# An odd layer's latent projections as three products of fp32r parts in place of float32 products

## The reference

```python
c_q, c_kv, k_r = jnp.split(t @ w_in, (MLA_Q_LORA, MLA_Q_LORA + MLA_KV_LORA), axis=-1)
...
return jnp.split(_heads(c_q @ w_uq, MLA_HEADS, MLA_NOPE_DIM + MLA_ROPE_DIM), (MLA_NOPE_DIM,), axis=-1)
...
k_nope, v = jnp.split(_heads(c_kv @ w_ukv, MLA_HEADS, MLA_NOPE_DIM + MLA_V_DIM), (MLA_NOPE_DIM,), axis=-1)
k_shared = jnp.broadcast_to(k_r[:, None], k_nope.shape[:-1] + (MLA_ROPE_DIM,))
...
y = _merge_heads(_dense_attention(q[:, :, None], k, v, kc, vc, MLA_SCALE)[:, :, 0]) @ w_out
```

## Time and profile before

| | us |
|---|---|
| median of 3 runs (2413.46 to 2417.34) | 2415.53 |
| the profiled execution, its own time | 2413.82 |
| its span | 2412.4 |
| PE busy (matmul) | 2257.8 |
| DVE busy | 1271.6 |
| ACT busy | 1074.9 |
| mean granted clock of TensorE, share of full speed | 0.973 |

### The profile page before, as it was taken

The page is one execution under the profiler, slowest core; times in us unless marked ns, Lnnn a source line. Parts: engine busy times, 40 slices in busy tenths (PEclk is TensorE's granted clock), DMA queues, the critical chain, the costliest instruction groups (busy, mean ns, idle before and its releaser), DMA issues.

```text
span 2412.4 us, 39225 instructions
## 1 busy us (share of the span) xinstructions
PE 2257.8 (94%) x17014; PEld 2017.2 (84%) x17014; DVE 1271.6 (53%) x1928; ACT 1074.9 (45%) x1691; POOL 54.2 (2%) x100
## 2 busy tenths in 40 slices
PE   6999979998999999989996989999999999998997
PEld 5998869997999799879995766888888886477997
DVE  3555566556555666365555326763444653446665
ACT  3444455445444554354435526552333451345553
POOL 0000100000000000000000000000000000000000
PEclk9999989999999999989998999999999999999998
DMA  7454625545554544245444121022223433204451
GB/s 313 175 192 184 228 107 206 195 170 197 185 200 166 205 188 166 108 183 189 183 158 193 70 74 49 1 105 87 88 101 126 158 123 136 74 18 156 165 200 39
DMA packets 51627, 353.58 MB, mean 147 GB/s; under 512 B 8064, under 2 KB 8448, under 8 KB 8832
## 3 DMA queue, kind: packets, MB, share of 16 engines
q1 hardware_dynamic: 47520, 346.05, 38.4%
q10 hardware_dynamic: 864, 4.63, 0.5%
q0 software_dynamic: 3072, 0.40, 0.1%
HBM read 349.61 MB, written 1.05 MB: 145 GB/s over the span
## 4 chain that ended last, share of the span: by engine, by line
PE 85%; DVE 8%; ACT 4%; DMA 1%; issue 1%; SPq 0%; POOL 0%; DVEq 0%; ACTq 0%
PE ps L683 13%; PE ps L685 13%; PE ps L684 13%; PE ps L818 5%; PE ps L2381 5%; PE ps L2383 5%; PE ps L2382 4%; PE ps L383 3%; PE ps L384 2%; PE ps L385 2%; PE ps L2111 2%; PE ps L2112 2%; PE ps L2113 2%; PE ps L1347 1%; PE ps L884 1%; PE ps L871 1%
## 5 line engine op out<-in xcount | busy, mean ns | idle before, releaser
L358 DVE TENSOR_TENSOR wl<-ring,wh 128x1024 fp32r<-128x1024 f32 x406 | 477.5, 1221 | 276.0 <-ACT wh L353 275.4
L683 PE MATMUL ps<-xs,wh 128*128 128x256 f32 x1760 | 504.5, 287 | 24.8 <-DVE wl L358 13.9
L684 PE MATMUL ps<-xs,wl 128*128 128x256 f32 x1760 | 503.2, 286 | 0.0
L685 PE MATMUL ps<-xs,wh 128*128 128x256 f32 x1760 | 503.1, 286 | 0.0
L353 ACT ACTIVATE wh<-ring 128x1024 fp32r<-128x1024 f32 x406 | 405.1, 1050 | 177.8 <-PE ps L685 128.0
L683 PEld LDWEIGHTS ps<-xs,wh 128*128 128x128 f32 x1760 | 343.6, 195 | 28.3 <-issue 18.9
L684 PEld LDWEIGHTS ps<-xs,wl 128*128 128x128 f32 x1760 | 343.4, 195 | 0.0
L685 PEld LDWEIGHTS ps<-xs,wh 128*128 128x128 f32 x1760 | 343.2, 195 | 0.0
L683 PE MATMUL ps<-hh,wh 128*128 128x256 f32 x880 | 249.1, 283 | 0.7 <-DVE hl L784 0.7
L684 PE MATMUL ps<-hh,wl 128*128 128x256 f32 x880 | 249.0, 283 | 0.0
L685 PE MATMUL ps<-hl,wh 128*128 128x256 f32 x880 | 249.0, 283 | 0.0
(11 more groups left out here) (426 smaller groups left out, 4004.5 us busy)
## 6 DMA issues: line engine op xcount, KB each, us to landing
ring<-wstream SPq DMA_DIRECT2D x329, 1024.0 KB, 4.9
ada_rows<-ada_stage POOLq DMA_DIRECT2D x96, 4.0 KB, 4.3
CN<-consts ACTq DMA_DIRECT2D x1, 1136.0 KB, 15.7
X<-xin ACTq DMA_DIRECT2D x1, 1024.0 KB, 10.7
X<-cin ACTq DMA_DIRECT2D x1, 1024.0 KB, 9.2
out<-X SPq DMA_DIRECT2D x1, 1024.0 KB, 3.9
PT__65<-pin ACTq DMA_DIRECT2D x1, 512.0 KB, 18.9
ab_w<-wab ACTq DMA_DIRECT2D x1, 512.0 KB, 3.7
```

The lines of the kernel that those rows point to most:

```text
L358: dve.tensor_tensor(lo, tile_of(i), hi.bitcast(F32), ALU.subtract).then_inc(low_part, 1)
L683: pe.matmul(out, wh[:, w, c, :], x_hi, start=start, stop=False, skip_group_check=True)
L684: pe.matmul(out, wl[:, w, c, :], x_hi, start=False, stop=False, skip_group_check=True)
L685: return pe.matmul(out, wh[:, w, c, :], x_lo, start=False, stop=True, skip_group_check=True)
```

## The change

- The x half's norm no longer writes `H` but parts: `act_x_high` makes the high part of a tile and a new `act_whole` the whole value, both on ACT, two instructions a tile where one stood; DVE subtracts (`dve_modulated_low`, L579 of the old file). The context half's norm is split in the same way, with the whole value on DVE.
- The 13 weight slots of `l1_in`, `l1_uq` and `l1_ukv` are split slot by slot: `act_m_high(s)` on ACT, `dve_m_low(s)` on DVE, the latter into the ring slot. Slots 0 to 3, 11 and 12 have 2048 columns, slot 4 has 256, slots 5 to 10 have 1536. From slot 6 on, and for slots 2 to 4, the high part waits for the products of an earlier slot. Slots 0 and 1 are split among the last feed-forward pieces, slots 2 to 6 among the `l1_in` tiles, 7 to 12 among the `l1_uq` tiles and the rotary chain.
- The scaled latents are split too: three ACT copies and one DVE subtraction for `c_q`, two copies and one subtraction for `c_kv`. ACT comes to the two copies behind the second query tile, and DVE waits for them before it turns and spreads `k_r`.
- PE forms three fp32r products where it formed one in float32, over the same chunks and tiles; the sums of squares, the rotations, the attention and `l1_out` stay in float32.

The diff, cut to its core:

```diff
-           "l0_1x": "l0_x", "l0_1c": "l0_c", "l1_1": "l1"}
+           "l0_1x": "l0_x", "l0_1c": "l0_c", "l0_2x": "l1_x", "l0_2c": "l1_c", "l1_1": "l1"}
...
-            if name in ("l0_1x", "l0_1c"):
+            if name[0:2] == "l0":
...
-            for c in (2 * q, 2 * q + 1):
+            for c in (2 * q, 2 * q + 1) if name != "l0_2x" else ():
...
+        M_SLOTS = ([("l1_in", j, 2 * KC * P) for j in range(4)] + [("l1_in", 4, KC * ROPE)]
+                   + [("l1_uq", j, 12 * P) for j in range(6)] + [("l1_ukv", j, 2 * KC * P) for j in range(2)])
+        m_wh = [put("m_wh", [2, SLOT], F32R, ("big", 16384)), put("m_wh1", [1, SLOT], F32R, ("Z", 8192)),
+                put("m_wh2", [2, SLOT], F32R, ("XH", 0))]
+        m_w_high, m_w_low = sem("m_w_high"), sem("m_w_low")
+
+        def m_load(s):
+            return FIRST[M_SLOTS[s][0]] + M_SLOTS[s][1]
+
+        def m_high(s):
+            k, j = (0, s % 2) if s < 5 else (1, 0) if s == 5 else (2, s % 2)
+            return m_wh[k][:, j, 0:M_SLOTS[s][2]]
+
+        def m_low(s):
+            return ring_low[:, m_load(s) % RING, 0:M_SLOTS[s][2]]
+
+        def m_parts(s, kc, width):
+            return (w[:, 0:kc * width].rearrange("p (c m) -> p c m", c=kc) for w in (m_high(s), m_low(s)))
+
+        def act_m_high(s):
+            act.wait_ge(*loaded(m_load(s)))
+            if s < 2:
+                act.wait_ge(f_low, NPAIR + 7)
+            elif s == 5:
+                act.wait_ge(*x_split("l1_c"))
+                act.wait_ge(x_high, x_parts("l1_c") + 4)
+            else:
+                act.wait_ge(raw_done, FREED[m_load(4 if s == 6 else s - 2)][1])
+            act.activation(m_high(s), slot(m_load(s))[:, 0:M_SLOTS[s][2]], ACT.Copy).then_inc(m_w_high, 1)
+
+        def dve_m_low(s):
+            dve.wait_ge(m_w_high, s + 1)
+            dve.tensor_tensor(m_low(s), slot(m_load(s))[:, 0:M_SLOTS[s][2]], m_high(s).bitcast(F32), ALU.subtract
+                              ).then_inc(m_w_low, 1)
...
-                    act_modulated("l0_2x", 2 * (k - 6))
-                    act_modulated("l0_2x", 2 * (k - 6) + 1)
+                    for c in (2 * (k - 6), 2 * (k - 6) + 1):
+                        act_x_high("l0_2x", c)
+                        act_whole("l0_2x", c)
+                if k in (7, 9):
+                    act_m_high(k // 8)
...
+            act.activation(x_whole(name, c), Z[:, ln_half(name), c, :], ACT.Identity, scale=g, bias=b).then_inc(low_whole, 1)
...
+                if k >= 7:
+                    dve_modulated_low("l0_2x", k - 7)
+                if k == 9:
+                    dve_m_low(0)
...
             dve_pair("l0_2c", 3, z + 16)
+            dve_m_low(1)
...
+            def tile(s, at, M, b, kc, hi, lo, N, width):
+
+                w_hi, w_lo = m_parts(s, kc, width)
+                pe.wait_ge(m_w_low, s + 1)
+                for c in range(kc):
+                    pe.matmul(ps[0:M, b, 0:N], w_hi[:, c, at:at + M], hi(c), start=(c == 0), stop=False)
+                    pe.matmul(ps[0:M, b, 0:N], w_lo[:, c, at:at + M], hi(c), start=False, stop=False)
+                    mm = pe.matmul(ps[0:M, b, 0:N], w_hi[:, c, at:at + M], lo(c), start=False, stop=(c == kc - 1))
+                mm.then_inc(raw_done, 1)
...
+            pe.wait_ge(*x_split("l1_x"))
+            for t in range(6):
+                tile(t // 2, (t % 2) * P, P, bank_cq(t), KC, half(0), half(1), T, 2 * P)
             pe.wait_ge(*m_a.at("cq5"))
-            total(m_cq_sq, 6, T, 4, "sum0")
-            pe.wait_ge(h_made, 2 * KC)
-            pe_raw_tiles("l1_in", 3, 2, KC, both, 2 * T, lambda t: 2 + t)
-            pe_raw_tiles("l1_in", 4, 1, KC, both, 2 * T, lambda t: 0, per_slot=1, M=ROPE)
+            total(m_cqs, 6, T, 4, "sum0")
...
+            for t in range(2):
+                tile(3, t * P, P, 2 + t, KC, both(0), both(1), 2 * T, 2 * P)
+            tile(4, 0, ROPE, 0, KC, both(0), both(1), 2 * T, ROPE)
...
-            pe_raw_tiles("l1_uq", 0, 8, 6, lambda c: m_cq[:, c, :], T, bank_qn)
+            cq = lambda part: lambda c: part[:, c, :]
+            for t in range(8):
+                tile(5 + t // 2, (t % 2) * P, P, bank_qn(t), 6, cq(m_cqh), cq(m_cql), T, 2 * P)
...
+                tile(11, t * P, P, bank_kn(t), 2, cq(m_ckvh), cq(m_ckvl), 2 * T, D)
+            w_hi, w_lo = m_parts(12, 2, D)
+            pe.wait_ge(m_w_low, 13)
...
+                if t == 1:
+                    act_m_high(2)
                 if t == 2:
                     act_factor("l0_2c")
+                    for c in range(4):
+                        act_x_high("l0_2c", c)
+                if t == 3:
+                    act_m_high(3)
+                    for c in range(4, KC):
+                        act_x_high("l0_2c", c)
+            act_m_high(4)
             rsqrt(0, T)
+            act_m_high(5)
+            act.wait_ge(*m_v_.at("cq"))
+            for q in range(3):
+                act.activation(m_cqh[:, 2 * q:2 * q + 2, :], m_cqw[:, 2 * q:2 * q + 2, :], ACT.Copy).then_inc(*m_a(f"cqh{q}"))
...
+            act_m_high(6)
             rsqrt(1, 2 * T)
             for t in range(8):
                 act.wait_ge(*raw_tile("l1_uq", t))
                 act.activation(m_q[0:NOPE, 2 * t, :], ps[0:64, t % 4, 0:T], ACT.Copy,
                                scale=m_scale).then_inc(*m_a(f"qn{t}"))
+                if t == 1:
+                    act.wait_ge(*m_v_.at("ckv"))
+                    for c in range(2):
+                        act.activation(m_ckvh[:, c, :], m_ckvw[:, c, :], ACT.Copy).then_inc(*m_a(f"ckvh{c}"))
+                if t % 2:
+                    act_m_high(7 + t // 2)
             for t in range(4):
                 act.wait_ge(*raw_tile("l1_uq", 8 + t))
                 act.activation(m_qr[:, t, :], row(t % 4), ACT.Copy, scale=m_scale).then_inc(*m_a(f"qr{t}"))
+                if t % 2:
+                    act_m_high(11 + t // 2)
...
-            dve_layer_norm("l0_2c")
-            for c in range(KC):
-                g, b = ln_cols("l0_2c", c)
-                dve.wait_ge(z_normed, 4 * LNS.index("l0_2c") + c // 2 + 1)
-                dve.tensor_scalar(H[:, 1, c, :], Z[:, 1, c, :], g, b, ALU.mult, ALU.add).then_inc(h_made, 1)
-            for i, (name, dst, N, n, gain) in enumerate((("cq", m_cq, T, 6, "cq_gain"),
-                                                         ("ckv", m_ckv, 2 * T, 2, "ckv_gain"))):
+            for q in range(4):
+                dve_centre("l0_2c", q)
+            for q in range(4):
+                dve_square_pair("l0_2c", q)
+            dve_m_low(2)
+            dve_scaled("l0_2c", 0)
+            dve_scaled("l0_2c", 1)
+            dve_modulated_low("l0_2c", 0)
+            dve_scaled("l0_2c", 2)
+            dve_modulated_low("l0_2c", 1)
+            dve_m_low(3)
+            dve_scaled("l0_2c", 3)
+            dve_modulated_low("l0_2c", 2)
+            dve_modulated_low("l0_2c", 3)
+            dve_m_low(4)
...
+                if name == "cq":
+                    dve_m_low(5)
+                    dve.wait_ge(*m_a.at("cqh2"))
+                    dve.tensor_tensor(m_cql[:, :, :], m_cqw[:, :, :], m_cqh[:, :, :].bitcast(F32), ALU.subtract
+                                      ).then_inc(*m_v_("cql"))
+                    dve_m_low(6)
+                else:
+                    dve.wait_ge(*m_a.at("ckvh1"))
+                    dve.tensor_tensor(m_ckvl[:, :, :], m_ckvw[:, :, :], m_ckvh[:, :, :].bitcast(F32), ALU.subtract
+                                      ).then_inc(*m_v_("ckvl"))
...
+                if t % 2:
+                    dve_m_low(7 + t // 2)
+            dve_m_low(11)
...
+                if t == 1:
+                    dve_m_low(12)
```

More of the change, by code:

```diff
@@ L2688, in pe_odd_mixer @@
         def pe_odd_mixer():
-            pe.wait_ge(h_made, KC)
-            half, both = lambda c: H[:, 0, c, :], lambda c: H[:, :, c, :]
             def total(sq, n, N, b, name):
@@ L2695, in total @@
                 mm.then_inc(*m_p(name))
+            def tile(s, at, M, b, kc, hi, lo, N, width):
[6 more added lines that the diff above has]
+                mm.then_inc(raw_done, 1)
+            half = lambda part: lambda c: xc[:, 0, c, part, :]
+            both = lambda part: lambda c: xc[:, :, c, part, :]
             def bank_cq(t):
@@ L2728, in bank_qr @@
                 return t % 4
-            pe_raw_tiles("l1_uq", 4, 4, 6, lambda c: m_cq[:, c, :], T, bank_qr)
+            for t in range(4):
+                tile(9 + t // 2, (t % 2) * P, P, bank_qr(t), 6, cq(m_cqh), cq(m_cql), T, 2 * P)
             for t in range(4):
@@ L2739, in bank_kn @@
                 return t % 4
-            pe_raw_tiles("l1_ukv", 0, 8, 2, lambda c: m_ckv[:, c, :], 2 * T, bank_kn, per_slot=8)
-            n = FIRST["l1_ukv"] + 1
-            w = slot(n).rearrange("p (c m) -> p c m", c=2)
-            pe.wait_ge(*loaded(n))
+            for t in range(8):
+                tile(11, t * P, P, bank_kn(t), 2, cq(m_ckvh), cq(m_ckvl), 2 * T, D)
```

(5 more changed lines are left out.)

60 lines of the change are left out of this document (32 added, 28 removed).

## The result

The changed kernel takes 2417.68 us (median of 20 runs, 2415.15 to 2421.11), the kernel before beside it on the same chip 2413.48 (20 runs). The ratio is 1.0022, 95% interval 1.0015 to 1.0029: slower by about 4 us. The forecast was slower, 2422.5 in a range of 2414 to 2430; in the difference it said +7.0. Of the 4.8 us by which the forecast's time lies too high, 2.0 are its base: it counted from the median of three runs, 2415.53, and the twenty give 2413.48.

A forecast was written before the change was run, and what follows sets the result against it. PE, with 85% of the chain, was taken as the bound. Steps 1 to 6 summed to +1.0 us, the clock added +6.0; +7.0 on 2413.8 gave 2420.8, plus 1.7 to the runs' median 2422.5, range 2414 to 2430.

The forecast's parts named there:

- Step 1: Last feed-forward pieces: added ACT instructions and slot high parts lengthen the four steps, +7.6 us without the clock.
- Step 2: c_q tiles: shorter products give -3.5 us, a longer wait before the sum of squares +2.0, together -1.5.
- Step 3: Three tiles of 512 tokens: shorter products with the parts ready in time, -4.4 us.
- Step 4: Query tiles: products -5.4 us, but PE waits 6.8 for slot 7's low part from DVE, together +1.4.
- Step 5: Wait before the fifth key tile: slot 12's low part stands inside DVE's rotary chain, +2.2 us.
- Step 6: Key tiles 5 to 8 and value tiles: twelve tiles at 1.36 us instead of 1.72, -4.3 us.
- Step 7: Clock falls behind new waits: 1.2 us last pieces, 1.6 sum of squares, 3.2 slot 7; +6.0, bounds 0 to 12.8.
- the clock holds: Rival: clock holds or its falls are hidden, at most one fall, +1.0 to +4.7 us, 2416.5 to 2420; chance 0.23.
- the forecast's own case: Whole kernel: slower by +4.9 to +10 us, chance 0.47.
- PE stays the bound: Rival: new ACT and DVE work fits idle time if slot 7's low part starts within 8.6 us; about -13.5, 2402; chance 0.13.
- the four terms: Shorter products alone, in c_q, 512-token, query, and key and value tiles: 6 x 0.58 + 3 x 1.47 + 12 x 0.45 + 16 x 0.36.

The follow-up runs named there:

- e3: Changed kernel with the full-precision copy of the x half's norm made by DVE again instead of ACT: 2415.19 us, ratio 1.0000 to the kernel before.
- e4: Changed kernel with ACT making the norm parts of a pair one piece later than it is scaled: 2409.74 us, ratio 0.9981 to the kernel before.
- e9: Changed kernel with only the high parts of slots 0 and 1 moved to the last two pieces: 2422.04 us, ratio 1.0039 to the kernel before.
- e5: Changed kernel with 75 unread PE products added in the waits before the fifth query and fifth key tiles: 2414.54 us, ratio 1.0001 to the kernel before.
- e2: Changed kernel with slot 12's low part moved from DVE's rotary chain to behind the fourth key copy: 2417.22 us, ratio 1.0010 to the kernel before.
- e1: Changed kernel with the spread of k_r cut into four pieces behind the low parts of slots 7 to 10: 2416.69 us, ratio 1.0012 to kernel before.
- e8: Changed kernel reordered in the query and key tiles only, last pieces and c_q tiles left alone: 2408.89 us, ratio 0.9974 to the kernel before.
- e7: Changed kernel with all reorderings, from the last feed-forward pieces through the key tiles: 2394.15 us, ratio 0.9913 to the kernel before.
- e6: Kernel before (float32 products) with ACT shifting a pair one piece later and two key copies between the query rotations: 2403.31 us, ratio 0.9951.
- e10: e7 with each query tile turned once the next has run, and slot 11's low part behind the first rotation: 2393.87 us, ratio 0.9922 to kernel before.

## Why the prediction was right, and where it was off

The forecast was right in sign and range, and right in its reason: shorter products are given back in waits of PE for ACT and DVE. By its steps:

*Step 1. Last pieces, +7.6 and 1.2 of clock.* Measured +8.9, and steps of 5.44, 7.24, 5.44 and 5.76 us where 5.4, 7.3, 5.4 and 5.8 were forecast. PE's waits in them were put too long (4.4, 2.6 and 2.9; they are 2.0, 2.7, 0.8 and 2.7), because pieces at the lower clock took 4.6 us where one takes 3.1; the steps do not depend on it. The low parts of DVE at the start and the end of the four steps, which answer to rows 6:

```profile
1957.22 0.69 DVE L2634 TENSOR_TENSOR fl<-f_hidden,fh 128x512 fp32r<-128x512 f32 x1 [3.07 <-ACT fh L2529]
...
1981.10 0.69 DVE L2634 TENSOR_TENSOR fl<-f_hidden,fh 128x512 fp32r<-128x512 f32 x1 [1.67 <-ACT fh L2529]
```

23.9 us in place of 16.3. ACT in the second step, which answers to rows 5:

```profile
1965.47 0.60 ACT L622 ACTIVATE xc<-Z,ln_col 128x256 fp32r<-128x256 f32 x1 [1.90 <-DVE Z L555]
1965.98 0.59 ACT L2571 ACTIVATE xc_whole<-Z,ln_col 128x256 f32<-128x256 f32 x1
...
1967.45 1.89 ACT L2390 ACTIVATE m_wh<-ring 128x2048 fp32r<-128x2048 f32 x1
1969.25 0.61 ACT L2529 ACTIVATE fh<-f_hidden 128x512 fp32r<-128x512 f32 x1
```

ACT's wait of 1.90 us is as long as before, although ACT has up to 2.8 us more to do in the step: in a ring the idle time does not shrink when work is added. e3, e4 and e9 show it from three sides.

*Step 2. `c_q` tiles, -1.5.* Measured -1.5, with the wait of 2.7 us that was forecast.

*Step 3. Tiles of 512 tokens, -4.4.* Measured -4.5. Here stood the first excess of the clock: I had added half a fall, 1.6, and none came.

*Step 4. Query tiles, +1.4 and 3.2 of clock.* Measured +3.2 in all. The wait was forecast as 6.8 and is 6.9, and the chain in order of time shows the links that were named:

```profile
2036.91 0.62 ACT m_ckvh L2875
2037.62 1.23 DVE m_ckvl L2928
...
2040.10 4.42 DVE m_k L2937
2044.55 0.77 DVE m_q L2941 x2
2045.32 1.68 DVE ring_low L2394
```

The fall behind it cost 1.25 us (e5), not 3.2. This is **the term that was mis-sized**: I took the price of the fall at the keys before the change. A fall is paid only while PE runs. The stretches at 0.50, split where PE goes on, first at the keys before the change:

```profile
2068.10:2069.00 0.90, 0.00 (x1) 0.03 (x1) 0.87 (x3) 0.00 (x0) 0.00 (x0) 0.52 0.00 0
2069.00:2074.95 5.95, 5.95 (x7) 2.47 (x8) 2.37 (x4) 0.59 (x1) 0.00 (x0) 0.50 0.01 3
```

Then at slot 7 and at the keys of the changed kernel:

```profile
2043.15:2047.13 3.98, 0.00 (x0) 0.03 (x1) 3.95 (x5) 0.00 (x0) 0.00 (x0) 0.50 0.30 126
2047.13:2049.95 2.82, 2.82 (x13) 2.82 (x14) 2.20 (x3) 0.00 (x0) 0.00 (x0) 0.50 0.03 6
2077.25:2079.66 2.41, 0.00 (x1) 0.03 (x1) 2.30 (x7) 0.00 (x0) 0.00 (x0) 0.50 0.00 0
2079.66:2084.10 4.44, 4.44 (x11) 3.48 (x12) 2.42 (x4) 0.59 (x1) 0.00 (x0) 0.50 0.00 0
```

PE ran 5.95, 2.82 and 4.44 us at the lower level; half of that, 3.0, 1.4 and 2.2, is near the prices of 3.2, 1.25 and 2.0. At slot 7 the other 4.0 us of slow time lay inside the long wait and cost nothing. The form of the products makes little of the difference: in e4 the same products behind the same wait ran 5.67 us at 0.50 and the fall cost 2.5, and at the keys they ran 6.03 us at it for a price of 2.7, where float32 products paid 3.2 for 5.95.

*Step 5. Wait for keys, +2.2.* Measured +2.2; e2 takes just this away.

*Step 6. Key and value tiles, -4.3.* Measured -4.7, made of two things. A tile of parts takes (17.76 - 0.69) / 12 = 1.42 us at full clock in e5, not 1.36, which gives -3.6. And the fall that was there before cost 3.2 and now costs 2.0, which I had not counted: -1.1.

*Step 7. The clock, +6.0.* Measured, against the kernel before: +1.4 in the last pieces (e1 has two falls there where the changed kernel has a third, and starts the `c_q` tiles 1.4 us earlier), 0 behind the sum of squares, +1.25 at slot 7, and -1.1 at the keys: +1.5, so 4.5 less than forecast. The key and value tiles' pace (0.7) and about 0.5 in the query tiles went the other way, and together that is the difference between +7.0 and the +3.6 of the trace.

Behind the wait of 2.7 half a fall was counted, and a fall comes or it does not. Eight profiled executions have this wait, with the same instructions behind it: in the changed kernel, e2, e4 and e5 the clock held, in e1, e3, e8 and e9 it fell, for 1.6, 1.7, 2.9 and 3.0 us. e9, whose `c_q` tiles start when they do in the changed kernel and which had the fall, has a stretch 6.9 us longer than before. That this is almost the +7.0 of the forecast is in part luck: its fall behind the sum of squares cost 3.0 where 1.6 was counted, the one at slot 7 1.5 where it was 3.2.

The Trainium skill ("TensorE: Matmul & The Clock Gate", section "What's actually happening") puts the cost of running up to full clock at under 1% of a typical kernel's span, and says not to fit it to a particular count of slow products. As to leaving the term out for that: the sum without it was +1.0, with it +7.0, and the trace shows +3.6. e5 shows that leaving it out is wrong here, by 3.3 us for two falls where the whole question was 4 us. These two are 0.14% of the span; what all falls of the kernel cost was not measured.

Of the rivals, "the clock holds" has the measured size in its range (+1.0 to +4.7; 2416.5 to 2420), which the forecast's own case (+4.9 to +10) does not. But it does not hold as a mechanism: the clock did fall in the last pieces, at slot 7 and at the keys, and only its price was small. "PE stays the bound" was named with the right condition. It is what e7 makes true by another order, and its gain on the kernel before is 19.7 us of stretch, where the products alone had been put at 19.1 (the four terms give 19.0). That the two agree is chance, since half of the gain came from waits and a fall that the float32 kernel had as well, and 8.2 us of waits remain.

What was not tried: which of the added instructions' places would be best if the halves of the norm were split otherwise, and what brings the clock down behind a wait of 2.7 us in one execution and not in another.

## What to carry to other kernels

Before giving work to an engine that looks idle, look for a ring: if the engine's idle time ends at another engine in every step, and that engine waits for it in turn, the idle time is no room, and each instruction added in its line counts in full (e3: 0.9 to 1.0 us a step), while one that lies beside it on the other engine costs nothing. Taking one dependence one step later (e4, two lines) opens it, and is worth trying before the work is moved or made less. Where a change shortens PE and lengthens what feeds it, write out the feeding engine's order from the last thing PE gave it to the first thing PE needs: long instructions that are needed late, like the spread of 4.4 us, belong in pieces behind those that are needed soon. And test such a change only once the order has been adapted to it; here the same products were worth +4 us in one order and -9 in another.

## What was not expected of the hardware

- A wait of 2.7 us between two dense stretches of PE brought the clock down to 0.50, the 1.2 GHz level, in four profiled executions of eight, and one of 2.4 us did in e1. Waits up to 1.8 us brought no fall in e6, e7, e8 (behind the second sum of squares) and e10. But in the last pieces of the changed kernel a wait of 2.05 us was followed by a fall 1.1 us after PE had gone on, so the length of the one wait does not decide alone.
- A fall's price is about half the slow time in which PE runs, not a fixed sum: 3.2 us at the keys before the change, 2.0 there now, 1.25 behind the wait of 6.9 us, and 2.5 behind the same wait in e4.
- Products that nobody reads, put into a wait, hold the clock at 1.00 and are worth 3.3 us of stretch here at no cost, since they end before the wait does.
